# Index keys turned by pairs, attention outputs turned whole, stored rows ahead of key groups, and value pages on two queues, in a two-layer decoder step

## The reference

```python
# layer 0: 12 heads, 2 kv heads, an indexer picks the tokens
q, k, v, qi, ki, wi, qm = split(h @ w_in_a)
s_ix = relu(qi . ki_all) summed over 16 index heads by wi     # ki_all: cache_a_ik pages + new
sel  = top_k(s_ix)
so   = softmax(q . k[sel] - alibi) @ v[sel]                    # cache_a_k, cache_a_v
# layer 1: 12 heads, 4 kv heads, cumulative forget bias
so   = softmax(q . k_all + c_q - c_k) @ v_all                  # cache_b_k, cache_b_v
# both layers
mo   = softmax(qm . mem_k) @ mem_v                             # 4 heads, 256 memory tokens
h = layer_norm(alpha * h + concat(so, mo) @ w_o)
h = layer_norm(alpha * h + hier_moe(h))
```

## Time and profile before

| what | us |
|---|---|
| time before, median of 3 runs | 2137.57 (2133.9 to 2138.18) |
| the profiled execution | 2131.57 |
| its span | 2129.8 |
| TensorE busy in the span | 2047.3 (96%) |
| VectorE busy | 773.1 (36%) |
| ScalarE busy | 387.6 (18%) |
| GpSimd busy | 25.6 (1%) |
| mean DMA rate over the span | 304 GB/s |

### The profile page before, as it was taken

The page is one execution under the profiler, slowest core; times in us unless marked ns, Lnnn a source line. Parts: engine busy times, 40 slices in busy tenths (PEclk is TensorE's granted clock), DMA queues, the critical chain, the costliest instruction groups (busy, mean ns, idle before and its releaser), DMA issues.

```text
span 2129.8 us, 33851 instructions
## 1 busy us (share of the span) xinstructions
PE 2047.3 (96%) x13356; PEld 1291.9 (61%) x13356; DVE 773.1 (36%) x1278; ACT 387.6 (18%) x932; POOL 25.6 (1%) x43
## 2 busy tenths in 40 slices
PE   8999998999999999999989999899999999999998
PEld 7778886888744435353478867566886344343434
DVE  0229998601752221212330433441138312122223
ACT  1220103500421101010221100342024111010122
POOL 0000002100000000000000000000000000000000
PEclk9999999999999999999999999999999999999999
DMA  9834579964279999999944778899631999999994
GB/s 283 247 119 150 177 252 295 312 235 157 80 292 426 422 429 418 428 426 426 392 139 125 285 277 297 319 386 382 232 132 57 423 426 418 427 414 425 418 427 181
DMA packets 210787, 647.43 MB, mean 304 GB/s; under 512 B 55400, under 2 KB 84857, under 8 KB 181089
## 3 DMA queue, kind: packets, MB, share of 16 engines
q1 hardware_dynamic: 194497, 633.99, 77.2%
q10 hardware_dynamic: 14624, 7.48, 1.4%
q0 software_dynamic: 1536, 4.20, 0.6%
HBM read 639.62 MB, written 5.96 MB: 303 GB/s over the span
## 4 chain that ended last, share of the span: by engine, by line
PE 78%; DMA 11%; SPq 6%; issue 2%; DVE 2%; ACT 1%; ACTq 0%; DVEq 0%
PE bank L749 19%; PE bank L1452 15%; PE bank L1251 11%; PE bank L1499 9%; PE bank L1513 6%; DMA ring<-in_w_down 5%; SPq L427 4%; DMA ring<-in_w_up 4%; PE bank L1425 4%; PE bank L982 3%; DMA ring<-in_cache_b_k 1%; PE bank L1335 1%; PE bank L869 1%; SPq L424 1%; PE bank L1222 1%
## 5 line engine op out<-in xcount | busy, mean ns | idle before, releaser
L1452 PE MATMUL bank<-ring,AT 128*64 128x512 f32 x2048 | 457.5, 596 | 12.2 <-DMA ring<-in_w_up 9.0
L749 PE MATMUL bank<-X,ring 128*128 128x264 f32 x1664 | 387.3, 390 | 6.2 <-ACT X L1881 6.2
L749 PEld LDWEIGHTS bank<-X,ring 128*128 128x128 f32 x1664 | 313.1, 191 | 65.0 <-issue 13.3
L1452 PEld LDWEIGHTS bank<-ring,AT 128*64 128x64 f32 x2048 | 144.0, 137 | 286.3 <-issue 278.8
L1625 ACT ACTIVATE arena<-bank 128x512 f32<-128x512 f32 (+9 forms) x307 | 135.5, 479 | 735.2 <-PE bank L749 252.3
L1499 PE MATMUL bank<-ring,arena 128*64 128x512 f32 x1024 | 224.4, 594 | 18.7 <-ACT arena L1625 13.8
L2601 DVE TENSOR_TENSOR X<-bank,X 128x264 f32<-128x264 f32 x256 | 110.7, 432 | 361.8 <-PE bank L1513 359.8
L1251 PE MATMUL bank<-AT,ring 128*128 128x264 f32 x1024 | 232.3, 390 | 0.0
L1251 PEld LDWEIGHTS bank<-AT,ring 128*128 128x128 f32 x1024 | 196.6, 192 | 34.0
L1499 PEld LDWEIGHTS bank<-ring,arena 128*64 128x64 f32 x1024 | 73.2, 137 | 159.5 <-issue 147.6
L2209 DVE STREAM_TRANSPOSE ring<-ring 128x4096 f32<-128x4096 f32 x24 | 106.5, 4442 | 100.8 <-DMA ring<-in_cache_b_k 100.6
(11 more groups left out here) (361 smaller groups left out, 1344.8 us busy)
## 6 DMA issues: line engine op xcount, KB each, us to landing
ring<-in_w_gate SPq DMA_DIRECT2D x64, 2048.0 KB, 15.3
ring<-in_w_up SPq DMA_DIRECT2D x48, 2048.0 KB, 16.1
ring<-in_w_down SPq DMA_DIRECT2D x48, 2048.0 KB, 13.2
ring<-in_w_o SPq DMA_DIRECT2D x16, 2048.0 KB, 15.7
ring<-in_w_up SPq DMA_DIRECT2D x32, 1024.0 KB, 7.8
ring<-in_w_down SPq DMA_DIRECT2D x32, 1024.0 KB, 16.0
ring<-in_cache_b_k SPq DMA_DIRECT2D x128, 256.0 KB, 5.5
ring<-in_cache_b_v SPq DMA_DIRECT2D x128, 256.0 KB, 8.1
```

The source lines that it names most:

```text
L749: mm = pe.matmul(B[at + f][:, 0:n_tok], u[:, c * 512 + f * P:c * 512 + (f + 1) * P], src[8 * half + c][:, 0:n_tok], start=(half == 0 and c ...
L1452: mm = pe.matmul(B[bank][64 * s:64 * s + 64, :], M.xsT[:, at:at + 64], ring[slots[s][0]][:, c * FE:(c + 1) * FE], start=(half == 0 and c = ...
```

## The change

Seven edits:

- **Index keys.** The pages of samples 2s and 2s + 1 now lie side by side in SBUF (`index_key`), so one 128x128 transpose turns a page of both. `turn_cached` is 4 transposes a step.
- **Outputs.** `fold` becomes `turn_out`: whole 128x128 transposes of the copied tile into the bank, one for each kv or memory head; VectorE (`place_out`) sums the four groups of rows while it reads the bank, by small reductions straight into the attention output. As one bank serves all tiles, `turn_out(x)` waits for `place_out(x - 1)`. The new tokens' values go to columns of their own, and VectorE adds them at the end. The constants `fold6` and `fold4` go.
- **Stored rows.** The turns of `a.kT` stand ahead of key group 1, those of `a.memK` and `a.mvT` ahead of group 3; nothing stands inside a group in layer 1.
- **Value pages, layer 1.** SyncE issues 6 of the 8 pages of each value unit, GpSimd the last 2, with its wait for its own batch before; TensorE waits on `pool_in` ahead of the seventh page of every unit.
- **layer_norm.** `scale(0)` is four instructions of one chunk, each counted on its own.
- **Idle products.** Five stand between layer 0 and layer 1.
- **Constants** and the helper `diagonal` move.

```diff
--- before.py
+++ after.py
@@
-        u += units("v", range(16), 8, 3) + units("mv", range(2), 4)
+        u += units("v", range(16), 8 - POOL_PAGES // 2, 3) + units("mv", range(2), 4)
...
+def index_key(b, g):
+
+    return (b // 2 * PAGES + g) * P + b % 2 * 64
...
-                        if layer == 0:
-                            per -= POOL_PAGES
+                        per -= POOL_PAGES * per // PAGES
...
+                pool.wait_ge(S("table_in"), 16)
+                per = UNIT // a.W
+                own = POOL_PAGES * per // PAGES
+                for u in range(NB * PAGES // per):
+                    s, _, _, before = units[layer]["v", u]
+                    t = ring[s]
+                    b, first = divmod(u * per, PAGES)
+                    pool.wait_ge(free(layer, s), before)
+                    if layer or u:
+                        pool.wait_ge(S("pool_in"), 16 * (POOL_PAGES * NB * layer + own * u))
+                    load_pages(pool, vregs, S("pool_in"), b, first + per - own, own,
...
-                        for s in range(2):
-                            b = 2 * g + s
-                            keys, at = (a.IK, b * PAGES * 64) if b < IK_EARLY else (late[0], (b - IK_EARLY) * PAGES * 64)
-                            at += (4 * j + pg) * 64
-                            mm = pe.matmul(B[n % 2][64 * s:64 * s + 64, pg * P:(pg + 1) * P],
-                                           keys[:, at:at + 64], ident, start=True, stop=True)
+                        at = index_key(b, 4 * j + pg)
+                        mm = pe.transpose(B[n % 2][:, pg * P:(pg + 1) * P], keys[:, at:at + P], ident)
...
+                    if m == 1:
+                        new_values()
...
-                        if layer == 0 and pg == PAGES - POOL_PAGES:
-                            pe.wait_ge(S("pool_in"), 16 * POOL_PAGES * (b + 1))
+                        own = POOL_PAGES * per // PAGES
+                        if k == per - own:
+                            pe.wait_ge(S("pool_in"), 16 * (POOL_PAGES * NB * layer + own * (u + 1)))
...
-                def fold(x):
+                def turn_out(x):
                     pe.wait_ge(S("ov_copied"), 12 * layer + x + 1)
                     if x == 0:
                         pe.wait_ge(S("sm_turned"), 2 * layer + 2)
-                        new_values()
...
+                        pe.wait_ge(S("at_done"), 13 * layer + x)
+                    for g in range(a.nk if x < NB else HM):
+                        mm = pe.transpose(B[bank + 1][:, g * P:(g + 1) * P], a.ov[x % 2][:, g * P:(g + 1) * P], ident)
...
                     key_products(layer, a, 0)
                     slab(layer, "qm", 0, Xc, T, 0)
+                    early_rows(a.kT, a.nk, 3, T)
                     key_products(layer, a, 1)
                     slab(layer, "mkv", 0, Ac, SEQ, 0)
                     key_products(layer, a, 2)
                     slab(layer, "mkv", 1, Ac, SEQ, 0)
-                    key_products(layer, a, 3, lambda: late_rows(layer, a))
+                    early_rows(a.memK, HM, 2, SEQ)
+                    early_rows(a.mvT, HM, 2, SEQ)
+                    key_products(layer, a, 3)
...
                     layer_norm(layer, n_quad)
+                    idle_products(5)
...
+                def place_out(x):
+
+                    dve.wait_ge(S("ov_turned"), 12 * layer + x + 1)
+                    if x < NB:
+                        rows = turned[:, 0:a.W].rearrange("p (k g r) -> p k r g", g=4, r=32)
+                        for kv in range(a.nk):
+                            h = 8 + HALF * (x // 2) + kv * a.G % HALF
+                            made = dve.tensor_reduce(Av[:, kv * a.G:(kv + 1) * a.G, SEQ + x], rows[:, kv, h:h + a.G, :], AX.X, ALU.add)
...
+                    if n >= 4 and n % 2 == 0:
+                        place_out(n // 2 - 2)
+                for x in range(len(ITEMS) // 2 - 1, 12):
+                    place_out(x)
...
+                    made = dve.tensor_tensor(out, out, new[:, h:h + a.G, :], ALU.add)
...
-                scale(0)
+                for c in range(4):
+                    dve.tensor_tensor(Xc[c], Xc[c], M.rstd, ALU.mult).then_inc(S("ln_normed"), 1)
```

More of the change, by code:

```diff
@@ L804, in late_rows @@
                 at = other_banks(layer)
-                if layer == 1:
-                    for t in range(3):
-                        natural(a.kT, a.nk, t, at)
                 for src in (a.memK, a.mvT):
@@ L810, in late_rows, with early_rows @@
                         natural(src, HM, t, at, SEQ)
+            def early_rows(src, nh, n, col):
+                pe.wait_ge(S("slab_copied"), cnt["slab"])
+                for t in range(n):
+                    natural(src, nh, t, other_banks(1), col)
             def indexer(a):
@@ L1146, in new_values @@
                         own = p[:, kv // (a.nk // 2), :, 8:32].rearrange("b s (q i) -> b q s i", i=HALF)
-                        pe.matmul(out[:, kv], a.VNs[:, kv * P:(kv + 1) * P], own, start=(kv == 0), stop=False)
-                def fold(x):
+                        pe.matmul(B[bank][:, SEQ + 48 * kv:SEQ + 48 * (kv + 1)], a.VNs[:, kv * P:(kv + 1) * P], own,
+                                  start=True, stop=True)
+                def turn_out(x):
                     pe.wait_ge(S("ov_copied"), 12 * layer + x + 1)
@@ L2260, in prompt_attention @@
                 v2 = lambda x, w: x.rearrange("p (s k) -> p s k", s=2)[:, :, 0:w]
+                turned = B[key_banks(layer) + 1]
+                def place_out(x):
[5 more added lines that the diff above has]
+                            made = dve.tensor_reduce(Av[:, kv * a.G:(kv + 1) * a.G, SEQ + x], rows[:, kv, h:h + a.G, :], AX.X, ALU.add)
+                            if kv < a.nk - 1:
+                                link(made)
+                    else:
+                        m = x - NB
+                        for j in range(2):
+                            rows = diagonal(turned, 64 * j + HM * (2 * m + j), 0, P, [(P + 1, HM), (32, 2)])
+                            made = dve.tensor_reduce(Av[:, H:H + HM, SEQ + 2 * m + j], rows, AX.X, ALU.add)
+                            if j == 0:
+                                link(made)
+                    made.then_inc(S("at_done"), 1)
                 for n in range(len(ITEMS) + 1):
@@ L2296, in prompt_attention @@
                         e.then_inc(S("p_norm"), 1)
+                    if n >= 4 and n % 2 == 0:
+                        place_out(n // 2 - 2)
+                for x in range(len(ITEMS) // 2 - 1, 12):
+                    place_out(x)
+                dve.wait_ge(S("at_done"), 13 * layer + 12)
+                dve.wait_ge(S("p_out"), base + len(ITEMS))
+                for kv in range(a.nk):
+                    new = B[key_banks(layer)][:, SEQ + 48 * kv:SEQ + 48 * (kv + 1)].rearrange("p (b i) -> p i b", i=HALF)
+                    out, h = Av[:, kv * a.G:(kv + 1) * a.G, SEQ:T], kv * a.G % HALF
+                    made = dve.tensor_tensor(out, out, new[:, h:h + a.G, :], ALU.add)
+                    if kv < a.nk - 1:
+                        link(made)
+                made.then_inc(S("at_done"), 1)
             def router_weights(layer):
```

60 lines of the change are left out of this document (15 added, 45 removed).

## The result

The changed kernel is slower. Its median is 2146.3 us over 9 runs (2140.83 to 2151.5), that of the kernel before 2133.9 over 9 runs (2129.87 to 2138.18); the ratio is 1.0054, with a 95% interval from 1.004 to 1.0069. The forecast was 2124 with a range up to 2135, and 0.06 for slower. The profiled execution took 2147.73 us, its span is 2146.0, 16.2 more than before.

A forecast was written before the change was run, and what follows sets the result against it. TensorE, busy 96% of the span, was taken as the bound, with GpSimd's batches pacing the second layer's value stage. -7.8 - 2.0 - 3.9 + 0.1 = -13.6 gave 2118.0 us profiled, 2124 as a median, range 2112 to 2135.

The forecast's parts named there:

- index keys: Index stage: transposes of page pairs halve the turning instructions; 8 pairs of steps save 0.97 us each, -7.8 us.
- outputs, first layer: First layer's attention: whole transposes replace folds, less VectorE's reductions ahead of the next item; -2.0 us (0 to -5.4).
- start of layer two: Between the layers: idle products keep TensorE's clock full and quarter scaling brings first rows 0.9 us earlier; -3.9 us.
- key groups: Second layer: stored-row turns fit into the 2.75 and 3.43 us waits for keys, so the last group ends 5.9 us earlier.
- value stage and its end: Second layer's value pages: GpSimd paces TensorE, giving back the key groups' 5.9 us; +0.1 for both together.
- The 6.0 that was added for the median: Whole kernel: median of three timed runs, 2137.57 us, lies 6.0 above the profiled execution, 2131.57; added at the end.
- the cycle of GpSimd's batches: Second layer's value stage: time per GpSimd batch, 7.53 of the first layer less 1.16, taken as 6.4 us (5.4 to 7.9).
- the second rival: Second layer's value stage: GpSimd's cycle is long, 7.9 us; attention ends 24.1 later, sum +10.4, 2148 us; chance 0.06.
- GpSimd would have kept up: Second layer's value stage: cycle up to 6.0 us, DMA engines stay the limit; sum -19.7, 2118 us; chance 0.28.
- The low-clock rival: Last key group: 16 transposes in the wait don't hold TensorE's clock, +2.6 us, chains add 1.7; 2128 us; chance 0.10.
- The index saving: After the index stage: a rival had the saving lost in a later wait because VectorE's search ends too late; 2132 us; chance 0.05.
- The waits that the prediction named as its sign: TensorE at value products from about unit 7: some 2 us each for the forecast, under 1 or over 3 for rivals.

The follow-up runs named there:

- index_by_page: The changed kernel without the split of value pages, with the 8 products of 64 columns an index step again: 2127.8 us, ratio 0.9972 to the kernel before.
- with_folds: The changed kernel without the split of value pages, with the folds of before in place of the turned outputs: 2115.0 us, ratio 0.9905 to the kernel before.
- no_split: The changed kernel with all value pages of the second layer back on SyncE's queue: 2118.9 us, ratio 0.9938 to the kernel before.
- rows_late: The changed kernel without the split of value pages, with all stored rows back in the middle of group 3: 2120.7 us, ratio 0.9937 to the kernel before.
- split_only: The kernel before with only the quarter of the second layer's value pages moved to GpSimd's queue: 2165.0 us, ratio 1.014 to the kernel before.
- depth2: The changed kernel with GpSimd's second-layer batches on two semaphores in turn, so two may be under way: 2115.3 us, ratio 0.9909 to the kernel before.
- one_page: The changed kernel with GpSimd issuing 1 and SyncE 7 of each second-layer unit's 8 value pages: 2131.8 us, ratio 0.9985 to the kernel before.
- light_queue: The changed kernel with only 2 of SyncE's 6 value pages a unit loaded in the second layer: 2121.7 us in one run.
- rows_group2: The changed kernel without the split of value pages, with the new keys' row turns ahead of group 2, not 1: 2118.3 us, ratio 0.9916 to the kernel before.
- no_idle_five: The changed kernel without the split of value pages and without the five idle products: 2119.9 us, ratio 0.9939 to the kernel before.

## Why the prediction was wrong, step by step

| step | forecast | measured | from |
|---|---|---|---|
| index keys | -7.8 | -8.9 (trace -8.3 to -8.5) | index_by_page |
| outputs, first layer | -2.0 | -1.8 at full clock | 65.8 to 64.0, with_folds and no_split |
| start of layer two | -3.9 | -3.9 in the trace | 28.3 to 24.4 |
| key groups | -5.9 | -2.0 | 127.8 to 125.8 |
| value stage and its end | +6.0 | +29.8 | 110.4 to 140.2 |

The measured column adds up to +13.2; the medians differ by 12.4, the spans by 16.2. The 6.0 that was added for the median was too much as well: over nine runs the kernel before is 2.3 above its profiled execution, not 6.0.

**The step that failed is the cycle of GpSimd's batches,** the term "Two issues fewer are 2 x 0.58 = 1.16 less; the bytes are the same, so nothing else is taken off", which put c at 6.4 us; it measured 7.67. The place, the wait and the form of the sum were right, and the second rival (2148) is near what happened. I had weighed it at 0.06. With c = 7.67 the forecast's own formula puts the end of the attention at 1374.0 + 16 x 7.67 = 1496.7 and the sum at +6.7, 2144.

The error was this one subtraction. In the first layer of the kernel before, the eight batches take 5.5 to 7.8 us from first issue to last landing, 6.5 on average; in the second layer of the changed kernel 6.55. Both carry 512 KB. The two issues did go: the last page is now issued 0.6 us behind the first, not 1.8, and the chain above runs through this issue. But this last page then took 5.95 us on average from its issue to its landing, where it took 4.70, and that gives the 1.2 us back. The issues of GpSimd's value pages, first layer before and second layer changed (tile, engine, count, size of one, median us from issue to landing):

```profile
ring<-in_cache_a_v POOLq DMA_DIRECT2D x32, 128.0 KB, 3.6
ring<-in_cache_b_v POOLq DMA_DIRECT2D x32, 256.0 KB, 5.6
```

A page has twice the bytes here, and the DMA engines are fuller (share 1.04 from 1360 to 1410, and 0.91 from 337 to 390 before). Which of the two makes how much of the longer landing was not separated. The hop of some 1.2 us from the landing to the next issue (table read, registers) stands on top in both layers. So the mean of 7.53 without a correction would have forecast the loss: 7.53 is beyond the break-even of 7.25 that the prediction names.

The same rows stood for a stage that could bear it. In the first layer there are 8 units for 16 value steps of TensorE, GpSimd starts 26 us ahead of the first scores (337.16 in the earlier trace rows), and TensorE there waits for no value page at all. The second layer has twice as many units of the same 2 MB, and a chain of 16 links in place of 8 with no lead: 16 x (7.67 - 5.4) = 36 us of excess, of which the stage shows 29.8. No run gave the second layer such a lead, or took it from the first; that the lead hid the cost is read from the rows.

The estimate from the page "DMA: Bandwidth & Descriptors" of the Trainium skill (Anatomy of one DMA: 2.0 us and the bytes at 436 GB/s) gave 2.6 us for a page. Measured were 4.8 us for the first page of a batch beside full engines and 3.5 at a DMA share of 0.65 (first twelve batches of each). By that page GpSimd would have kept up; the measurement decides against it here.

**The rest of the 29.8.** From group 3's end to the first issue 0.5, 15 cycles 115.0, the last batch 8.6 (it meets the weight loads), the tail 16.0: 140.1. The forecast had 16 x 6.4 and 13.9 = 116.3. Of the 23.8 between them the cycle makes 20.3, the first issue and the long last batch 1.4, and the tail 2.1: TensorE's granted clock was half for 3.4 us of it, from 1478.0, and the chain through the bank took 4.4 where 3.6 to 4.0 was priced.

**The key groups** gave a third of the forecast. Here are the averages of the three kernels with late rows and of the eight with rows at groups 1 and 3, each from the end of one group to the end of the next. Group 3 went from 45.4 to 41.7 us, a gain of 3.8 (5.1 between the two profiled executions of the kernels before and changed). Group 2 went from 41.5 to 41.8. Group 1 went from 40.9 (40.3 to 41.9) to 42.3 (41.4 to 44.2), so it gave 1.4 back. Its wait for keys was 1.17 in rows_late (1.67 and 1.97 in the two kernels with rows at group 2), not the 2.75 of before, so the 1.33 of ScalarE's copy and the 1.53 of turns did not fit. The products behind it also stall in their middle. Why that wait is shorter than in the kernel before and in split_only (2.74) was not tested.

**The outputs of the first layer** were priced about right: 1.8 of 2.0, where the clock is the same. The 2.9 us by which this attention is shorter in the changed kernel than in the kernel before are mostly something else. Of them 2.6 went also in split_only, which has the folds. The profiled execution of before had two stretches at half the clock there, one of 3.4 us at 367.3 and one from 428.7 to its end (3.94 us for what takes 2.86).

**The low-clock rival** didn't come in group 3: with its 16 transposes in the wait, it ran at a granted clock of 1.00 in the changed kernel.

```profile
1341.00:1353.00 12.00, 11.61 (x274) 6.68 (x274) 2.90 (x10) 2.65 (x6) 0.04 (x1) 1.00 0.84 308
```

The index saving was not lost later either. The waits that the prediction named as its sign (some 2 us each for the forecast, over 3 for the second rival) did not tell the two apart: of the eleven, from the sixth unit on, five were 3.7 to 3.9 us and six 0.3 to 1.9, 2.5 on average. GpSimd's cycle, the other sign, did.

## What to carry to other kernels

A queue that waits for its own landing is a chain: its pace is the latency of a batch plus the hop back to the issue. Here fewer issues did not shorten it, and half the bytes brought it only to 0.8. The number of links counts as much as their length. Before such a split is taken over from a stage where it costs nothing, see whether a lead may have hidden it there (here 26 us and half as many links), and compare the cycle as it stands, without corrections, with the pace of the stage it goes to; a second semaphore, so that two batches are under way, took the whole loss away. And where the DMA engines are full, a second queue had nothing to win here: depth2 was no faster than no_split beyond their intervals.

## What was not expected of the hardware

- The first page of 256 KB of a batch on GpSimd's queue took 4.8 us from issue to landing beside full DMA engines, 3.5 with the engines at 0.65, and a batch of two 6.5 and 4.8 (first twelve batches). One page alone took 5.07. The first layer's pages of 128 KB took 2.6 to 4.1 for the first of a batch.
- TensorE stalls within the runs of small key products, with nothing in the profile that releases it: in group 1 behind exactly 164 products in the changed kernel, no_split, depth2, one_page and light_queue, for 2.24, 1.41, 1.68, 1.68 and 0.86 us; behind 177 in rows_late and rows_group2; and at other places in the other kernels. The same instruction each time where the place is the same, and another length. The kernel before has one such piece, 0.86 us in group 0. That supply of instructions is behind it fits the fixed place, but no run tested it; it stays open.
- The granted clock fell to half for stretches of 3.4 us or two or three times that. At the start of the second layer it fell in the kernel before, split_only and no_idle_five, and not in the other ten kernels, which all have the idle products. There it lasted 10.2 us in the kernel before and 6.8 in the other two.
